# A mixer and mixture-of-experts block on one core: rows of the experts picked and returned by 0/1 products on TensorE, with two sets of expert weights instead of three

## What is computed

```python
group_sel = jnp.argmax(group_logits, axis=-1)
top_p, top_i = lax.top_k(jax.nn.softmax(in_group, axis=-1), TOP_K_IN_GROUP)      # 2 of 8
expert_ids = group_sel[:, None] * EXPERTS_PER_GROUP + top_i
combine = ...one_hot(expert_ids, 32) * (group_w * top_p)...
for e in range(N_EXPERTS):                                  # 32 experts
    hid = jax.nn.silu(t @ w_up1[e]) * (t @ w_up3[e])        # 1024 -> 512, twice
    y = y + combine[:, e:e + 1] * (hid @ w_down[e])         # 512 -> 1024
x = x + gt2 * rmsnorm(y, norm_gains[l, 3])
```

## Time and profile before

| | us |
|---|---|
| median of 3 runs | 1136.94 (1136.05 to 1137.46) |
| the profiled execution | 1133.66 |
| its span on the core | 1131.9 |
| first `expert_up` starts | 628.6 into the span |
| last `expert_down` ends | 1111.67 (1108.02 + 3.65) |
| PE busy | 992.9 (88%) |
| DVE, ACT, POOL busy | 428.2, 287.3, 178.7 |
| bytes moved by DMA | 281.67 MB |

### The profile page before, as it was taken

How to read it: one execution, slowest core, us unless ns; L and a number is a source line. 1 busy time by engine, 2 the same in 40 slices (tenths; PEclk the granted TensorE clock), 3 DMA queues, 4 the chain that set the end, 5 groups by cost and what they waited for, 6 DMA issues and landing times.

```text
span 1131.9 us, 17069 instructions
## 1 busy us (share of the span) xinstructions
PE 992.9 (88%) x7067; PEld 552.4 (49%) x7067; DVE 428.2 (38%) x853; ACT 287.3 (25%) x447; POOL 178.7 (16%) x239
## 2 busy tenths in 40 slices
PE   3999999999998999999997899977777788777876
PEld 2588478755556676546884433323322232222222
DVE  2477858444467341127437222222211221122124
ACT  3343462366641222245352000000000000000004
POOL 0100000322320100222601112211111111111002
PEclk9899999999999999999998899999999999999999
DMA  9676204205220002334329999999999999999996
GB/s 338 231 248 223 104 3 146 75 24 189 86 75 2 3 5 77 123 124 165 149 112 380 367 398 401 400 399 401 402 410 412 407 406 398 406 399 397 411 415 242
DMA packets 70803, 281.67 MB, mean 249 GB/s; under 512 B 9347, under 2 KB 18861, under 8 KB 46171
## 3 DMA queue, kind: packets, MB, share of 16 engines
q1 hardware_dynamic: 63408, 265.94, 60.6%
q0 software_dynamic: 5120, 8.40, 2.3%
q10 hardware_dynamic: 2218, 6.52, 1.6%
HBM read 276.62 MB, written 12.60 MB: 256 GB/s over the span
## 4 chain that ended last, share of the span: by engine, by line
PE 42%; SPq 30%; DVE 11%; DMA 8%; ACT 4%; issue 3%; POOL 1%; ACTq 0%; DVEq 0%; POOLq 0%
SPq L444 21%; PE ps L1718 7%; SPq L448 6%; PE ps L2042 4%; SPq L452 3%; PE ps L1729 3%; DMA ring<-in_w_up 2%; PE ps L2057 2%; PE ps L1587 2%; PE ps L1588 2%; PE ps L1589 2%; DMA arena<-in_w_mod 2%; PE ps L1830 2%; PE ps L1972 1%; DMA ring<-in_w_mod 1%
## 5 line engine op out<-in xcount | busy, mean ns | idle before, releaser
L2042 PE MATMUL ps<-arena 128*64 128x512 f32 x672 | 151.8, 596 | 35.1 <-DMA arena<-in_w_up 35.1
L1475 DVE TENSOR_TENSOR arena<-arena,ps 128x256 f32<-128x256 f32 x32 | 13.5, 421 | 370.6 <-ACT arena L988 370.6
L1718 PE MATMUL ps<-arena,ring 128*128 128x512 f32 x256 | 118.6, 604 | 0.0
L2042 PEld LDWEIGHTS ps<-arena 128*64 128x64 f32 x672 | 48.8, 137 | 136.6 <-issue 104.5
L2042 PE MATMUL ps<-ring,arena 128*64 128x512 f32 x352 | 79.9, 597 | 19.6 <-DMA ring<-in_w_up 19.6
L2057 PE MATMUL ps<-arena 128*64 128x512 f32 x336 | 78.4, 609 | 19.4 <-DMA arena<-in_w_down 14.2
L988 ACT ACTIVATE arena<-ps 128x256 f32<-128x256 f32 x32 | 12.3, 384 | 264.3 <-PE ps L2042 264.3
L1587 PE MATMUL ps<-h_upper,w_upper 128*128 128x512 f32 (+1 forms) x184 | 74.3, 404 | 4.4 <-POOL h_lower_first L573 4.1
L1589 PE MATMUL ps<-h_upper,w_lower 128*128 128x512 f32 (+1 forms) x184 | 72.7, 395 | 0.0
L1718 PEld LDWEIGHTS ps<-arena,ring 128*128 128x128 f32 x256 | 46.1, 190 | 48.8 <-issue 47.2
L1470 DVE TENSOR_SCALAR arena<-ps,par 128x64 f32<-128x64 f32 x256 | 67.2, 335 | 2.6 <-PE ps L2031 2.6
(11 more groups left out here) (388 smaller groups left out, 1605.8 us busy)
## 6 DMA issues: line engine op xcount, KB each, us to landing
arena<-in_w_up SPq DMA_DIRECT2D x84, 1024.0 KB, 28.8
ring<-in_w_up SPq DMA_DIRECT2D x44, 1024.0 KB, 29.1
ring<-in_w_down SPq DMA_DIRECT2D x11, 2048.0 KB, 35.0
arena<-in_w_down SPq DMA_DIRECT2D x11, 2048.0 KB, 32.4
arena<-in_w_down SPq DMA_DIRECT2D x20, 1024.0 KB, 28.4
ring<-in_w_mod SPq DMA_DIRECT2D x6, 2048.0 KB, 8.7
arena<-in_w_mod SPq DMA_DIRECT2D x6, 2048.0 KB, 9.4
ring<-in_w_in SPq DMA_DIRECT2D x6, 2048.0 KB, 8.4
```

The costliest lines, as they stand in the source:

```text
L1718: last = mm(ps[:, bank, :], w[:, k, P * (n % 2):P * (n % 2) + P], hT[:, k, :], start=(k == 0), stop=(k == KD - 1))
L2042: last = mm(ps[64 * hf:64 * hf + 64, UP_BANK[u], :].rearrange("p (m n) -> p m n", m=2), hgT[:, k, :], up_pair(u, k)[:, :, 256 * hf:256 * h ...
```

## The change

Rows no longer go through memory. ACT keeps the normalized rows on chip as a rounded part `n_hi`, and DVE the rest as `n_lo` (`lower_rows`); both are in the format of the one-pass products (float32r). DVE builds a matrix `pick` of zeros and ones (512 tokens by 256 slots of four blocks), and PE's `gather` multiplies: the stationary operand is a 128 x 128 piece of `n_hi` or `n_lo`, the moving one is 256 columns of `pick`; the result is already turned. Four blocks form a turn (TURN = 4). During a turn's four blocks PE gathers the next turn's rows, 16 products in each block, ACT and DVE take them out of PSUM (`turned_rows_low`, `turned_rows_high`).

Results go back in the same way. ACT and DVE split the weighted result of a block into an upper and a lower part (`yo_upper`, `yo_lower`), DVE builds a 0/1 matrix `back` (128 rows by 512 tokens, `back_rows`), and PE multiplies them, for each of the four groups of 128 tokens two products of 512 columns (`send_back`) into one pair of PSUM banks. DVE adds that pair to a sum `acc` in SBUF (`add_back`) before PE may write the pair again. The four pairs of block u are placed inside `expert_up` and before `expert_down` of block u + 1.

The tables in memory, the indirect DMAs, the read-back and the weighing at the end are gone. The room for the third set of weights is gone too (NSET = 2). The final sum, norm and output work on `acc`; x1 is put together again from `n_hi` and `n_lo` by POOL and scaled back by ACT.

The diff, cut to what the prediction speaks of:

```diff
-NSET = 3
-LOOPED = 30
-MAXO = 18
-MAXB = LOOPED + MAXO + (E - LOOPED)
-NOWHERE = 4096
+NSET = 2
+TURN = 4
+MAXO = 16
+MAXB = E + MAXO
...
-            with sp.Fori(0, LOOPED // NSET - 1) as it:
+            with sp.Fori(0, E // NSET - 1) as it:
...
                 act.wait_ge(rstd2, t + 1)
-                if t >= 2:
-                    act.wait_ge(h2_stored, 16 * t)
-                link(A(h2tok[:, t % 2, :], x1[:, t, :], ACT.Copy, scale=V("rs", 8 + t)))
-                act.dma_start(h2_dram[P * t:P * t + P, :], h2tok[:, t % 2, :]).then_inc(h2_stored, 16)
+                A(n_hi[t], x1[:, t, :], ACT.Copy, scale=V("rs", 8 + t)).then_inc(n_hi_ready, 1)
...
+            def expert_act(u, it, more):
+                act.wait_ge(up_done, TURN * it + (u + 1))
+                A(sil, ps[:, UP_BANK, 0:256], ACT.Silu).then_inc(sil_ready, 1)
+                if more and u == TURN - 1:
+                    turned_rows_low(it + 1)
+                if u == 0:
+                    act.wait_ge(w_now_ready, it + 1)
+                act.wait_ge(down_done, TURN * it + (u + 1))
+                y = yo[u % 2]
+                for a, h in ((0, 0), (HD, 512)):
+                    last = A(y[a:a + HD, h:h + 512], ps[a:a + HD, DOWN_BANK, :], ACT.Copy, scale=w_now[a:a + HD, u:u + 1])
+                last.then_inc(yo_upper, 1)
...
+            def lower_rows(t):
+                dve.wait_ge(n_hi_ready, t + 1)
+                dve.wait_ge(x1T_done, t + 1)
+                STT(n_lo[t], x1[:, t, :], V("rs", 8 + t), n_hi[t].bitcast(F32), ALU.mult, ALU.subtract).then_inc(n_lo_ready, 1)
             for t in range(NT):
+                if t >= 2:
+                    lower_rows(t - 2)
...
+            def pick_rows(turn, first=False):
+                if not first:
+                    dve.wait_ge(pick_step, 2 * turn)
+                for t in range(NT):
+                    ins = TS(pick[:, t, :], K("iota"), key[:, t:t + 1], None, ALU.is_equal)
+                ins.then_inc(pick_step, 1)
+                dve.wait_ge(pick_step, 2 * turn + 1)
+                for t in range(NT):
+                    ins = STT(pick[:, t, :], K("iota"), key[:, NT + t:NT + t + 1], pick[:, t, :].bitcast(F32), ALU.is_equal, ALU.add)
+                ins.then_inc(pick_ready, 1)
+                dve.wait_ge(pick_ready, turn + 1)
...
+            for c in range(2):
+                TT(key_diag[:, c], K("ident").rearrange("p (o q) -> p o q", o=1).broadcast_to((P, NT, P)),
+                   o1(key[:, NT * c:NT * c + NT]).broadcast_to((P, NT, P)), ALU.mult).then_inc(diag_ready, 1)
+            pick_rows(0, True)
+            lower_rows(3)
...
+            def add_back(t):
+                TT(two(acc[:, t, :]), two(acc[:, t, :]), ps[:, BACK_BANK:BACK_BANK + 2, :], ALU.add).then_inc(back_added, 1)
...
+            def yo_lower(u, it):
+                dve.wait_ge(yo_upper, TURN * it + (u + 1))
+                y = yo[u % 2]
+                for a, h in ((0, 0), (HD, 512)):
+                    o = HD - a
+                    last = STT(y[o:o + HD, h:h + 512], ps[a:a + HD, DOWN_BANK, :], w_now[a:a + HD, u:u + 1],
+                               y[a:a + HD, h:h + 512].bitcast(F32), ALU.mult, ALU.subtract)
+                last.then_inc(yo_ready, 1)
...
+            def back_rows(u, it):
+                b = back[u % 2]
+                if u == 0:
+                    dve.wait_ge(back_step, turn_steps * it + 1)
+                TS(b, key_rows[:, 0, :], slot_key[:, u:u + 1], None, ALU.is_equal).then_inc(back_step, 1)
+                dve.wait_ge(back_step, turn_steps * it + (2 * u + 2))
+                ins = STT(b, key_rows[:, 1, :], slot_key[:, u:u + 1], b.bitcast(F32), ALU.is_equal, ALU.add)
+                ins.then_inc(back_step, 1)
+                if u == TURN - 1:
+                    dve.wait_ge(back_step, turn_steps * it + turn_steps)
+                    TS(slot_key, slot_key, float(TURN * CAP), None, ALU.add).then_inc(back_step, 1)
+            def before_added(u, it, t):
+                dve.wait_ge(back_done, NT * (TURN * it + (u - 1)) + (t + 1))
+                add_back(t)
+            def expert_dve(u, it, more):
+                back_rows(u, it)
+                if u:
+                    for t in range(NT - 1):
+                        before_added(u, it, t)
+                dve.wait_ge(sil_ready, TURN * it + (u + 1))
+                TT(hid, sil, ps[:, UP_BANK, 256:512], ALU.mult).then_inc(hid_ready, 1)
+                if more and u == TURN - 1:
+                    turned_rows_high(it + 1, 2)
+                dve.wait_ge(ht_done, TURN * it + (u + 1))
+                CP(hidT, ps[:, DOWN_BANK, 0:256]).then_inc(ht_ready, 1)
+                if u:
+                    before_added(u, it, NT - 1)
+                if more and u == TURN - 1:
+                    turned_rows_high(it + 1, 3)
+                    pick_rows(it + 2)
+                yo_lower(u, it)
...
+            with dve.Fori(0, again) as it:
+                for u in range(TURN):
+                    expert_dve(u, it, True)
+                for t in range(NT):
+                    before_added(TURN, it, t)
+            for u in range(TURN):
...
+            def gather(u, parts, first=True, last=True):
+                for k in (2 * u, 2 * u + 1):
+                    for i, part in enumerate(parts):
+                        for t in range(NT):
+                            ins = mm(ps[:, u, 256 * (k % 2):256 * (k % 2) + 256], turned(part[t], k), pick[:, t, :],
+                                     start=(first and i == 0 and t == 0 and k == 2 * u), stop=(last and i == len(parts) - 1 and t == NT - 1),
+                                     skip_group_check=True)
+                if last:
...
+            def send_back(u, t, bank):
+                for h in range(2):
+                    ins = mm(ps[:, bank + h, :], back[u % 2][:, P * t:P * t + P], yo[u % 2][:, 512 * h:512 * h + 512], start=True,
+                             stop=True)
+                return ins
+            def before_back(u, it, t):
+                if t == 0:
+                    pe.wait_ge(yo_ready, TURN * it + u)
+                pe.wait_ge(back_added, NT * (TURN * it + (u - 1)) + (t + 1))
+                send_back(u - 1, t, BACK_BANK).then_inc(back_done, 1)
...
+                    if back_of is not None and k in (2, 4, 6):
+                        before_back(back_of, it, k // 2 - 1)
...
+            with pe.Fori(0, again) as it:
+                turn_of(it, True)
+                expert_up(0, it, it + 1, 0, 2 * it + 3, TURN)
+                before_back(TURN, it, NT - 1)
```

474 lines of the change are left out of this document (181 added, 293 removed).

## The result

| | before | after |
|---|---|---|
| median of 4 runs each, us | 1136.50 | 1249.05 |
| lowest to highest | 1136.05 to 1137.46 | 1247.41 to 1249.79 |
| profiled span | 1131.9 | 1245.6 |
| first up starts | 628.6 | 632.1 |
| up starts to last down ends | 483.1 | 590.0 |

The ratio is 1.0987, 95% interval 1.0968 to 1.1006. The change makes the kernel slower, as forecast, but by 112.6 us and not by 25. The spans differ by 113.7 us: 3.5 in the start, 106.9 in the blocks, 3.3 in the tail.

A forecast was written before the change was run, and what follows sets the result against it. DMA bounds the kernel before, PE with its waits for DVE after. Blocks +25.4 (508.5 against 483.1), start +1.4, tail -1.8 give +25.0 us, a span of 1156.9; added to the median 1136.94: 1162 us, range 1150 to 1175.

The forecast's parts named there:

- 16 x 0.12 = 1.9 us for the gather: PE's gather in each block: 16 products at 0.12 us, 1.9 us, replacing 1.0 us of turning and wait: +0.9.
- The return pair: PE's two return products per group of 128 tokens, 0.23 us each, 0.46 a pair; eight products a block, 1.8 us.
- The split: Blocks two to four of a turn: ACT and DVE have the result split 2.7 us after up starts; PE waits 0.15.
- The first block: First block of a turn: late returns and a 1.3 us PE wait for `hid` make it 17.7 us; the others 15.4.
- The last turn: Last turn, without gather: the path over silu and `hid` (0.95 us) takes its place in three blocks, -2.8 us.
- The start: Before the first block: `pick` ready at 619.2, then 7.0 and 3.8 us of gather products; up starts at 630.0, +1.4.
- The tail: From the last down to the end of the span: 15.3 + 3.1 = 18.4 us instead of 20.2, -1.8.
- DVE's hand-overs hide: Rival: waits for DVE vanish in three blocks of a turn, the first takes 17.0; 1142 us, chance 0.15.
- PE's 14.8 holds everywhere: Rival: every block takes PE's 14.8 us without waits, eight turns 471 us; 1124 us, a gain, chance 0.08.
- Products overlap: Rival: return products hide half behind their neighbours, 28 us go; 1134 us, no change, chance 0.03.
- Hand-overs are dearer: Rival: some ten hand-overs per block cost 0.1 us more each, +20 to +32; 1182 us, chance 0.08.
- Two sets starve: Rival: weight loads come too late with two sets, leaving a gap per block; at 2 us 1195 us, chance 0.06.

The follow-up runs named there:

- the run: Changed kernel with contiguous operands and reordered work, two gather products a block instead of 16, three of four returns left out inside the loop: 1121.8 us, ratio 0.9874.

## Why the prediction was wrong in size

The span came out 88.7 us above the forecast 1156.9: 81.5 in the blocks, 2.1 in the start, 5.1 in the tail.

**Right.** The direction, and the mechanism in the large: DMA stops being the bound, PE and its hand-overs with VectorE take over, the second queue's disappearance brings nothing. The floor of DMA, 15.05 us a block, is 14.9 in the run. The worst block of a turn is its first. A return product costs 0.23 us and not the 131 ns of the Trainium skill, "TensorE: Matmul & The Clock Gate", section "Back-to-back issue gap".

**The term that was mis-sized: "I take 0.12", 16 x 0.12 = 1.9 us for the gather.** It is 0.243 and 3.99 us. The bounds, 0.115 to 0.15, came from products whose stationary operands are contiguous, and the operand of the gather is not: its step of eight columns stands in the code of `turned`. With the contiguous operand the price is 0.12, as taken. The stretch from the first up to the end of the last down, forecast at 508.5 us, took 590.0, and 545.1 in the kernel with contiguous operands: the step is 45 of the 81.5 us. It is not 28 x 2.07 = 58, because in the first block of a turn a wait for `hid` lies under the gather. The rule that speaks against this change is that note on cachelines in the Trainium skill, "SBUF — State Buffer", section "Door 1: The DMA port swizzle"; I weighed another page's instead.

**The return pair, 0.46 us.** It is 0.66, and the up passes beside it lose 0.14 more, 0.34 a visit. I had 0.05 a joint as an upper end for the sum. The kernel with contiguous operands shows what that comes to: its blocks two to four still take 16.5 us and not 15.4, 1.1 x 21 = 23 us, and nearly all of it, 3 x 0.34 = 1.0 a block, is joints. The other 13 of the 36.6 us that remain there are in the first blocks and the last turn.

**The split, ready at 2.7.** It is ready at 3.34: ACT's two pieces take 1.38 and not 1.20, VectorE's 1.51 and not 1.38, the hand-overs the rest. The wait is 0.59 in place of 0.15. The second wait of my sum, 0.4 for the addition, is absent: the dearer returns and up's joints cover it. The two nearly cancel, so the 0.6 of the sum came out by luck. The absence of waits for `back_added` was one of the prediction's own signs of being wrong, and it came in three of four blocks; what is left is 0.3 us in the first block of a turn (2.1 us in 7 waits from 640 us on).

**The first block, 17.7.** It takes 19.3, and 18.5 with contiguous operands: the wait that I had priced at 1.3 us for `hid` lies under the longer gather, so that inside the loop PE never waits for `hid` (L1440), where the prediction had it wait; it came back as soon as the gather was short. The 0.8 that is left over 17.7 is the joints again. Two changes of order removed the whole excess over the other blocks. The order pieces had shown the cause rightly, but not that it would be hidden.

**The last turn, -2.8.** Its three later blocks were forecast at 14.5 each, and took 17.4, 15.6 and 15.7: the joints, and 1.8 more in the first of them. That 1.8 is PE's clock, which the prediction left at its upper level there. Without a gather PE waits 3.4 us for `hid` in the turn's first block, and the down products behind the wait take 5.44 us and not 3.65; the granted clock is 0.50, the lower level, in the stretch right behind their start:

```profile
1168.54 0.70 PE L2047 MATMUL ps<-cst,arena 128*128 128x128 f32 x2 [3.36 <-DVE arena L1440]
1169.86 5.44 PE L2057 MATMUL ps<-ring,arena 128*64 128x512 f32 x16 [0.61 <-DVE arena L1444]
```
```profile
1170.00:1172.00 2.00, 2.00 (x6) 0.50 0.79 332
```

**The start, 630.0.** 632.1. The first 32 products started 0.240 us apart at a granted clock of 0.50 (618 to 620 us), no more than the 0.243 in the loop at 1.00: with this layout half the clock cost nothing here. They took 7.8 us from 616.51, where I had 7.0 from 619.2. The lower part took 7.8 and not 3.8. That `pick` was ready 2.7 us sooner than forecast hides over half of it, and part of that is luck: in five other kernels with the same instructions up to there it was ready at 617.9 to 619.5.

**The tail, 18.4.** 23.5. Four of five us are VectorE's: I had taken 1.28 us for each scaling from the earlier trace rows, where it reads PSUM, and here it reads SBUF beside a busy POOL. The rest is the final returns at half the clock, 3.75 us for eight products, after PE had waited 3.2 us:

```profile
1226.00:1230.00 4.00, 3.12 (x8) 0.50 0.00 0
```

0.50 is the granted clock, the lower level of 1.2 GHz.

**The rivals.** None came. *DVE's hand-overs hide* was right on the addition and wrong on the split. *PE's 14.8 holds everywhere* fell by the gather. *Products overlap* was partly right on up, whose two halves start within 7 ns of each other (803.605 and 803.612), and wrong on the returns. *Hand-overs are dearer* pointed the right way, but had 0.1 us at ten joints as its worst. *Two sets starve* did not come: the weights of up landed 7.8 us after their issue.

## What to carry to other kernels

Before pricing a product by a row of the same shape, compare the layouts of both operands in SBUF: a stationary operand that puts only one element of fp32 on each 16 bytes cost twice the time here, and the remedy is in how it is stored, 8 bytes of step being free. When work is moved from DMA to an engine in small pieces between the pieces of another product, price the joints as well as the pieces. And a DMA share of 1.00 does not make DMA the bound: ask who waits for it.
